# Down products with the activations stationary and 512 weight columns moving, a shorter delta rule, and the first norm moved ahead

## What is computed (the reference, cut)

```python
for i in range(2):                       # block i
    mod = silu(c) @ w_ada[i] + b_ada[i]  # 6 vectors of 1024: shift, scale, gate twice
    x += g1 * mixer_i(rms_norm(x) * (1 + sc1) + sh1)       # hgrn2, then rg-lru
    x += g2 * peer_ffn(rms_norm(x) * (1 + sc2) + sh2)      # 16384 experts, top 16 of 8 heads
x = rms_norm(x)
# even layer: gated delta rule (6 heads of 128, chunks) + windowed attention -> w_out, layer norm
# conv ffn: up (1024 -> 2*2816), conv over time, silu gate, down (2816 -> 1024), layer norm
# odd layer: differential attention + gated linear attention, layer norm; conv ffn, layer norm
```

## Time and profile before

| | us |
|---|---|
| median of 3 runs (lowest, highest) | 3236.56 (3231.42, 3238.88) |
| the profiled execution's own time | 3236.47 |
| its span, first to last instruction | 3234.8 |
| PE busy, PEld busy | 3014.2, 2896.0 |
| DVE busy, ACT busy, POOL busy | 2230.7, 1585.7, 79.8 |
| share of the ending chain: PE, DVE, ACT | 80%, 5%, 4% |

### The profile page before, as it was taken

One profiled execution on the slowest core, in us unless ns is written; L12 is line 12 of the kernel. 1 busy time (PEld: TensorE's weight loads), 2 busy tenths in 40 slices (PEclk: granted clock), 3 DMA queues, 4 the chain that ended last, 5 costly groups with the idle time before them and its releaser, 6 DMA issues.

```text
span 3234.8 us, 64227 instructions
## 1 busy us (share of the span) xinstructions
PE 3014.2 (93%) x22954; PEld 2896.0 (90%) x22954; DVE 2230.7 (69%) x4709; ACT 1585.7 (49%) x3278; POOL 79.8 (2%) x121
## 2 busy tenths in 40 slices
PE   4997999999999999899999999998997889898898
PEld 4886899999999998799999999998986789886898
DVE  5336479888779974459888867775675358763686
ACT  1110457778544432555777744445442148461574
POOL 2000000000001100000000000001100000000000
PEclk9998999999999998999999999998997899997999
DMA  8520455454478852345444455554330045431453
GB/s 320 221 94 1 149 177 168 152 163 141 156 261 303 300 170 98 124 163 187 153 150 160 141 187 184 186 188 164 120 118 1 14 156 180 163 118 52 143 177 122
DMA packets 137769, 503.50 MB, mean 156 GB/s; under 512 B 15328, under 2 KB 15456, under 8 KB 137344
## 3 DMA queue, kind: packets, MB, share of 16 engines
q1 hardware_dynamic: 122544, 445.57, 41.2%
q0 software_dynamic: 15056, 55.65, 4.8%
HBM read 499.05 MB, written 2.10 MB: 155 GB/s over the span
## 4 chain that ended last, share of the span: by engine, by line
PE 80%; DVE 5%; ACT 4%; issue 1%; DVEq 0%; ACTq 0%
PE PB L509 12%; PE PB L511 12%; PE PB L510 12%; PE PA L509 9%; PE PA L511 9%; PE PA L510 9%; PE PB L499 5%; PE PA L685 4%; DVE w_low L1974 1%; PE PA L885 1%; PE PB L885 1%; PE PA L1025 1%; DVE BIG L2000 1%; PE PA L590 1%; PE PB L582 1%
## 5 line engine op out<-in xcount | busy, mean ns | idle before, releaser
L1062 ACT ACTIVATE w_high<-ring 128x512 fp32r<-128x512 f32 x1484 | 924.4, 630 | 944.3 <-PE PA L511 498.1
L1974 DVE TENSOR_TENSOR w_low<-ring,w_high 128x512 fp32r<-128x512 f32 x1484 | 1014.6, 695 | 430.3 <-ACT w_high L1062 411.9
L509 PE MATMUL PB<-h_high,w_low 128*128 128x256 f32 x3536 | 1024.6, 290 | 44.9 <-DVE h_low L1653 36.9
L511 PE MATMUL PB<-h_high,w_high 128*128 128x256 f32 x3536 | 1003.4, 284 | 0.0
L510 PE MATMUL PB<-h_low,w_high 128*128 128x256 f32 x3536 | 1002.7, 284 | 0.0
L509 PEld LDWEIGHTS PB<-h_high,w_low 128*128 128x128 f32 x3536 | 685.4, 194 | 60.6 <-issue 47.8
L509 PE MATMUL PA<-a_high,w_low 128*128 128x256 f32 x2400 | 678.7, 283 | 10.2 <-DVE a_low L1983 10.1
L511 PE MATMUL PA<-a_high,w_high 128*128 128x256 f32 x2400 | 676.8, 282 | 0.0
L510 PEld LDWEIGHTS PB<-h_low,w_high 128*128 128x128 f32 x3536 | 676.6, 191 | 0.0
L511 PEld LDWEIGHTS PB<-h_high,w_high 128*128 128x128 f32 x3536 | 675.6, 191 | 0.0
L510 PE MATMUL PA<-a_low,w_high 128*128 128x256 f32 x2400 | 674.6, 281 | 0.0
(11 more groups left out here) (326 smaller groups left out, 2849.4 us busy)
## 6 DMA issues: line engine op xcount, KB each, us to landing
ring<-tiles SPq DMA_DIRECT2D x842, 512.0 KB, 3.3
BIG<-ada POOLq DMA_DIRECT2D x96, 512.0 KB, 7.9
BIG<-skew POOLq DMA_DIRECT2D x4, 512.0 KB, 4.5
X<-x SPq DMA_DIRECT2D x1, 1024.0 KB, 5.8
skew<-BIG POOLq DMA_DIRECT2D x1, 1024.0 KB, 6.8
out<-X SPq DMA_DIRECT2D x4, 256.0 KB, 2.0
con<-consts SPq DMA_DIRECT2D x1, 853.0 KB, 8.7
BIG<-masks POOLq DMA_DIRECT2D x1, 768.0 KB, 8.0
```

Of the source, the lines that this page charges most:

```text
L509: mm(dst, lhs_l, high, start=start, stop=False, skip_group_check=True)
L511: return mm(dst, lhs_h, high, start=False, stop=stop, skip_group_check=True)
L1062: fn(tile_half(w_high, s, b), ring[:, at:at + HALF], ACT.Identity).then_inc(sem("high_ready"), 1)
L1974: tt(tile_half(w_low, s, b), ring[:, at:at + HALF], tile_half(w_high, s, b).bitcast(F32), ALU.subtract).then_inc(sem("low_ready"), 1)
```

## The change

1. `split_sums`: the activations (128 tokens of `a_high` or `a_low`) are stationary and 512 weight columns move, so a tile takes 12 matmuls, not 24; the sums then lie with tokens on the partitions. At each of the four ends ACT and DVE copy the sums to SBUF (`TMP`), PE turns them back in 16 transposes (`turn_sums`) into PB, and the additions to X read PB.
2. The modulation groups 8 to 11 are summed by PE after the norm that follows the first `peer`, groups 6 and 7 where all six were. At the start of the program the first norm's sums, root and scaling come before ada group 1.
3. Delta rule: beta is folded into a key decay made in the tile loop (rows of beta by PE at tile 3, copied by ACT at tile 4; masks applied on DVE at tiles 9 to 15), so the matrix needs no turning and beta scaling afterwards. Squares of q and k and v's turning move into tiles 38 to 40. A level makes three groups of products for each half g, not four (the last level two), because the second is had by swapping the operands. The mask DMA, `nbeta` and the buffers n, nt, c, p2 go. The output part that needs no second delta is made earlier.

The diff, cut to its core:

```diff
@@ banks of the norms
-            return (PB if name in SUMS else PA)[:, i * 512:i * 512 + T]
+            return PA[:, i * 512:i * 512 + T]
...
@@ PE
             def split_sums(j, k, it, step, first=False, last=False):
                 pe.wait_ge(sem("gated_ready"), it * 4 + (j + 1))
+                high, low = pair(a_high, j), pair(a_low, j)
                 for b in range(2):
                     pe.wait_ge(sem("low_ready"), it * (2 * step) + (2 * k + b + 1))
-                    for q in range(4):
-                        m = 4 * b + q
-                        ins = passes(PA[:, m * T:(m + 1) * T], k, b, q, pair(a_high, j), pair(a_low, j),
-                                     first and m % 2 == 0, last)
+                    w_h, w_l = tile_half(w_high, k, b), tile_half(w_low, k, b)
+                    for t in range(TT):
+                        dst, own = PA[:, (t * 2 + b) * HALF:(t * 2 + b + 1) * HALF], slice(t * P, (t + 1) * P)
+                        mm(dst, high[:, own], w_l, start=first, stop=False, skip_group_check=True)
+                        mm(dst, low[:, own], w_h, start=False, stop=False, skip_group_check=True)
+                        ins = mm(dst, high[:, own], w_h, start=False, stop=last, skip_group_check=True)
                     ins.then_inc((sem("mid_tile"), tile_done)[b], 1)
+            def turn_sums():
+                pe.wait_ge(sem("sums_copied"), w.up(sem("sums_copied"), TT))
+                for m in range(DC):
+                    for t in range(TT):
+                        ins = nc.tensor.transpose(PB[:, m * T + t * P:m * T + (t + 1) * P],
+                                                  TMP[:, t * D + m * P:t * D + (m + 1) * P], ident)
+                    if m % 2:
+                        ins.then_inc(sem("sums_turned"), 1)
...
-                    ada(LATER, 12, PB)
+                    ada(LATER, LATER + 2, PB)
                 for j in range(4 * steps + 1, NKEYS):
                     down(j)
+                turn_sums()
...
+                    if j == 3:
+                        beta_rows()
...
+                    if j == n - 4:
+                        pe.wait_ge(sem("attention_out_taken"), 4 * TT)
+                        gdn_squares(0)
+                    if j == n - 3:
+                        gdn_values()
+                    if j == n - 2:
+                        gdn_squares(1)
...
                 for lev in range(1, PAIR_LEVELS):
+                    last = lev == PAIR_LEVELS - 1
                     for g in range(2):
-                        pe.wait_ge(sem("inverse_step"), w.up(sem("inverse_step")))
-                        times(PA, g, "ct", "x").then_inc(sem("inv_p1"), 1)
-                        times(PB, g, "c", "y").then_inc(sem("inv_p2"), 1)
+                        if lev == 1:
+                            pe.wait_ge(sem("inv_p1_ready"), copied - 1 + g)
+                        pe.wait_ge(sem("inverse_x"), 2 * (lev - 1) + g + 1)
+                        times(gdn_bank(g), g, "ct", "x").then_inc(sem("inv_p1"), 1)
+                    if lev == 1:
+                        pair_products(4)
+                        pair_products(5)
                     for g in range(2):
                         pe.wait_ge(sem("inv_p1_ready"), w.up(sem("inv_p1_ready")))
-                        times(PA, g, "y", "p1").then_inc(sem("inv_xpx"), 1)
-                        pe.wait_ge(sem("inv_p2_ready"), w.up(sem("inv_p2_ready")))
-                        times(PB, g, "x", "p2").then_inc(sem("inv_ypy"), 1)
+                        if lev == 1:
+                            pe.wait_ge(sem("pair_taken"), 5 + g)
+                        pe.wait_ge(sem("inverse_y"), 2 * (lev - 1) + g + 1)
+                        if not last:
+                            times(gdn_bank(g), g, "y", "p1").then_inc(sem("inv_xpx"), 1)
+                        times(gdn_bank(2 + g), g, "p1", "y").then_inc(sem("inv_ypy"), 1)
...
-            ada(0, 2)
-            pe.wait_ge(sem("mod_ready"), w.up(sem("mod_ready")))
             rms()
+            ada(0, 1, PB, False)
+            ada(1, 2, PB)
+            pe.wait_ge(sem("mod_ready"), w.up(sem("mod_ready")))
...
             rms("experts0")
-            linear("lru_x", H, sem("h_ready"))
+            ada(LATER + 2, 12, PB[:, 1024:])
+            linear("lru_x", H, sem("h_ready"), 0, 2)
+            pe.wait_ge(sem("mod_ready"), w.up(sem("mod_ready"), 2))
+            linear("lru_x", H, None, 2)
@@ ACT
+            def copy_sums(stream):
+                r0, n = STREAM_AT[stream]
+                act.wait_ge(tile_done, r0 + n)
+                fn(TMP[:, 0:D], PA[:, 0:D], ACT.Identity).then_inc(sem("sums_copied"), 1)
...
                 for j in range(n):
+                    if j == n - 1:
+                        gdn_values()
+                        head_roots(2 * GDN_HEADS, 1.0, GDN_SUMS)
...
+                    if j == 4:
+                        act.wait_ge(sem("gam_psum"), w.up(sem("gam_psum")))
+                        fn(e["rows"], PA[:, 0:12 * P], ACT.Identity).then_inc(sem("beta_rows_taken"), 1)
...
@@ DVE
                 dve.wait_ge(tile_done, r0 + n)
+                v.tensor_copy(TMP[:, D:2 * D], PA[:, D:2 * D]).then_inc(sem("sums_copied"), 1)
                 for m in range(DC):
-                    add_chunk(m, PA[:, m * T:(m + 1) * T], gate).then_inc(sem("x_added"), 1)
+                    if m % 2 == 0:
+                        dve.wait_ge(sem("sums_turned"), w.up(sem("sums_turned")))
+                    add_chunk(m, PB[:, m * T:(m + 1) * T], gate).then_inc(sem("x_added"), 1)
...
+                    if j in (9, 12, 15):
+                        key_decay(j // 3 - 3)
+                    if j in (11, 14):
+                        query_decay(j // 3 - 3)
...
-            ada(0, 2)
-            modulate(0, 2)
+            ada(0, 1)
             dve.wait_ge(sem("x_loaded"), w.up(sem("x_loaded"), 16))
             rms(None, H)
+            ada(1, 2)
+            modulate(0, 2, PB)
```

More of the change, by code:

```diff
@@ L389, in build, with gdn_bank, gdn_part @@
         GDN_PSUM = {x: i + 1 for i, x in enumerate(
-            ("values", "matrix", "turned", "delta0", "carry", "delta1", "out"))}
-        GDN_COPIED = {x: i + 1 for i, x in enumerate(("values", "matrix", "turned", "delta0", "delta1"))}
+            ("values", "delta0", "carry", "early", "delta1", "out"))}
+        GDN_COPIED = {x: i + 1 for i, x in enumerate(("values", "delta0", "delta1"))}
+        GDN_PAIRS = (("k", 0, 0), ("k", 1, 1), ("k", 0, 1), ("q", 0, 0), ("q", 0, 1), ("q", 1, 1))
+        GDN_SUMS = PA[:, 1536:1536 + T]
+        HALF_HEADS = GDN_HEADS * P
+        def gdn_bank(i):
+            return (PA, PB)[i // 2][:, i % 2 * 1024:i % 2 * 1024 + HALF_HEADS]
+        def gdn_part(name, g):
+            return EVEN[name][:, g * HALF_HEADS:(g + 1) * HALF_HEADS]
         REL, ONEHOT, ROWS = big(0, 512), big(512, SKEW), big(105 * T, 4 * SKEW)
@@ L551, in all_taken, with ada @@
                 pe.wait_ge(taken, q0 + n)
-            def ada(first, last, dst=PA):
+            def ada(first, last, dst=PA, done=True):
                 pe.wait_ge(sem("ada_sums_ready"), last)
@@ L749, in mixing, with beta_rows @@
                     ins.then_inc(sem("ba_psum"), 1)
+                def beta_rows():
+                    pe.wait_ge(sem("beta_ready"), w.up(sem("beta_ready")))
+                    for t in range(TT):
+                        for h in range(GDN_HEADS):
+                            i = t * GDN_HEADS + h
+                            ins = mm(PA[:, i * P:(i + 1) * P], wide(e["beta"][:, i:i + 1], P, P), ident,
+                                     start=True, stop=True)
+                    ins.then_inc(sem("gam_psum"), 1)
                 def gam_columns():
+                    pe.wait_ge(sem("beta_rows_taken"), w.up(sem("beta_rows_taken")))
                     pe.wait_ge(sem("g_ready"), w.up(sem("g_ready")))
@@ L878, in even_mixer @@
[L878 to L886 removed]
+                    spread_roots(2 * GDN_HEADS, 2 * at, (i % 4) * 512)
@@ new lines, in pair_products @@
+                def pair_products(i):
+                    name, s, t = GDN_PAIRS[i]
+                    if i >= 2:
+                        pe.wait_ge(sem("pair_taken"), i - 1)
+                    for h in range(GDN_HEADS):
+                        ins = mm(gdn_bank(2 + i % 2)[:, h * P:(h + 1) * P],
+                                 e["k"][:, h * T + s * P:h * T + (s + 1) * P],
+                                 e[name][:, h * T + t * P:h * T + (t + 1) * P], start=True, stop=True)
+                    ins.then_inc(sem("pair_psum"), 1)
@@ new lines, in block, with times @@
+                def block(name, i):
+                    return e[name][:, i * P:(i + 1) * P]
+                def times(dst, g, lhs, rhs):
+                    for i in range(6):
+                        ins = mm(dst[:, i * P:(i + 1) * P], block(lhs, 6 * g + i), block(rhs, 6 * g + i),
+                                 start=True, stop=True)
+                    return ins
```

(21 more changed lines are left out.)

283 lines of the change are left out of this document (137 added, 146 removed).

## The result

The changed kernel takes 3159.46 us (median of four runs, 3159.38 to 3161.32) against 3235.12 for the kernel before on the same chip: a ratio of 0.9765, 95% interval 0.975 to 0.9781. It is faster, by 76 us where 122 were forecast, and lies 1.5 us above the range. The execution profiled took 3161.32 us, span 3159.6, so its rows are compared with a span of 3234.8 before: 75.2 us.

What follows compares the result with a forecast made beforehand. PE was taken as the bound, busy 93% of the span and 80% of the ending chain. Terms -64 + 8 - 7.5 - 7.5 - 52 = -123 took 3236.47 us to 3114; range 3093 to 3158.

Steps and rivals of the forecast that it cites:

- Down products: Down stages: 512-column fp32r matmuls start 216 ns apart (bounds 213, 225), saving 53 us outside and 11 in ada tiles: -64.
- the 11 ns: Down stages: a 256-column matmul takes 117.7 ns where streaming needs 106.7; this extra staying per matmul gave the 225 bound.
- Rival A: Down products: extra time goes with the columns, 512 take 233 ns, stage gains 9 us, not 64: 3169; chance 0.11.
- The ada tiles: 72 down tiles with ada work: DVE comes next as limit, 2.70 us a tile instead of 2.857, -11 us.
- Turning back: Four ends of the down stages: copies, four transposes before the first addition and semaphores cost +8 us (bounds 5 and 13).
- the 275 ns: Skill's price for a PE transpose; at it the ends would cost some 5 us more; six in 0.82 us were traced.
- Modulation sums: Around the first down stage's end: 32 records stay, 64 move behind the norm; net -7.5 us (bounds -13 and -2).
- Start: Program start: first norm's work goes before ada group 1, first product at 47.95 instead of 55.61; -7.5 us (bounds -9, -4).
- Delta rule: Even mixer: fewer passes before level 1, six product groups a level instead of eight, shorter tail; -52 us (bounds -62, -35).
- (a): Delta rule, end of the tile loop: squares and v's turning in tiles 38 to 41 delay the roots, +1.3 us.
- Rival B: Delta rule: low clock and waits take the place of its products, half of 52 gained: 3140; chance 0.12.
- Rival C: Down matmuls: stationary loads not hidden, about 111 ns each, 400 us, slower than before: 3514; chance 0.03.

Runs made afterwards that it cites:

- part 1 alone: The kernel before with only the 512-column down products and the sums turned back at the ends: ratio 0.9984 to the kernel before, -5 us.
- the bf16 series: Program of matmuls alone, without the kernel's computation, 512 bf16 columns back to back: 215.8 ns from start to start.
- the fp32r series: Same program of matmuls alone, 512 fp32r columns, both operands at even places: 226.7 ns from start to start, with or without busy neighbours.
- part 2 alone: The kernel before with only the first norm's work moved ahead and 64 of 96 later modulation-sum records moved behind the next norm: ratio 0.9937, -20 us.
- the all-even one: The changed kernel with only its buffers reordered, so weights, activations and normed input start at the same place modulo 2048 bytes: 3161.92 us, ratio 0.9767.

## Why the prediction was wrong, point by point

**Down products: the failed step is "I take 216 ns".** The bounds above it (213 and 225) missed, too. The plain float32 record that stood as its model has 2.8 ns above its 512 steps (216.1 alone); an fp32r matmul has 13.3 ns at even places, and the kernel's places add 4.5. The remark that the 11 ns might stay with each matmul was the right mechanism, though as a bound too low. Measured, by the same sum: 228 tiles x 0.05 and 72 x 0.034 give -14 us, not -64 (the four stages of part 1 alone: -13). The 15 ns by 3600 matmuls are 54 us, more than the whole miss; the other terms gave some of it back. What the places add is measured; where the constant of 13.3 ns comes from is not shown. Rival A named the right time for a stage (233 ns, 3169) and had 0.11, but not for its reason: the extra does not go with the columns. That it comes so near in the time is luck of the places.
The Trainium skill (TensorE: Matmul & The Clock Gate, "Back-to-back issue gap") gives 215.8 ns for 512 columns; the bf16 series agrees to the tenth, the fp32r series, at 226.7, does not.

**The ada tiles.** DVE was to end them at 2.70 us; it was PE at 2.82.

**Turning back.** +8 was forecast (bounds 5 and 13). The distances from last down matmul to mean squares grew by 2.08, 2.79, 2.63 and 2.99 us: +10.5, within the bounds. Four transposes take 0.67 us. A transpose's record is 0.27 us long but for the first of a group, and the starts lie 0.109 apart. So the 275 ns that the prediction quotes, and says that the trace disagrees with, fit the length of a record; as a pace, which the sum needs, they do not fit.

**Modulation sums.** -7.5 forecast; -6.9 in the run with part 2 alone and -8.0 in the changed kernel against part 1 alone (down stage 366.1 us for 379.5; from the end of the mean squares to the lru product 9.76 for 4.3 before). 64 records take 9.76 us and not 10.8. One step of it was luck: the 32 records left in the down stage were to be "over before the clock fell". In the run with part 2 alone they were (1192.92 to 1196.4), but the clock fell at once behind them, with the narrow down matmuls 213 ns apart until 1200.8. In the changed kernel it fell within them, and a dozen wide matmuls at 427 ns lost some 2.4 us (12 x 0.196). The sum has no term for either.

**Start.** 47.98 for 47.95. The sums of group 1 began at 42.72 for 42.55.

**Delta rule.** -52 forecast, -56 (between the down stages) to -57 (by the ratio) measured. By pieces in the changed kernel: mean squares to roots 203.3 us for 200.0, +3.3 where +2.3 was counted with the work in the loop; roots to level 1 19.2 for 51.4, -32.2 for -32; levels 49.5 for 68.8, -19.3, as worked out; the tail 21.9 for 30.8, -8.9 for -3. In the tail the output products behind the last copy fell from 4.3 to 1.62 us, the copy and squares from 2.95 to 0.82, and the spread roots on the chain from 4.98 (12 records) to 1.14 (4 records); for those the granted clock was 0.56 before and 1.00 after, so a part of this gain is the clock's. The prediction also has an error of 1.3 us in its sum: the -32 runs from the old start of level 1 to the new one (2475 to 2443) and so already holds the +1.3 of (a), which is added once more. Rival B is refuted: PE is not idle between the groups of a level, though the clock was low through the roots, as it supposed. Rival C too: loads stay hidden.

**The sum by measured terms:** -13 (down products) + 10.5 (ends) - 8 (sums) - 7.6 (start) - 57 (delta rule) = -75, for 75.2 between the two profiled executions and 76 between the medians.

## What to carry to other kernels

Price a matmul form by a series of exactly that type, width and pair of buffers; a record of another type is no model for it. In this case, halving the count of fp32r matmuls at even places saved a constant of 13 ns for each one saved, and no more. Then look at where the two operands of the hot matmuls start: here 32 bytes and an order of allocation, with no instruction changed, gave 17 us or more, where the wide form had given 3 to 5. Read a stage's distances one by one before you take its mean for a price: ten at the lower clock made 227.8 of 226.7.

## What was unexpected of the hardware

The distance between fp32r matmuls depends on where their operands lie against each other: 512 columns took from 226.7 to 233.4 ns, 256 columns from 115.6 to 120.0, at the same clock, alike each time a pair was run again. At the lower level neither the constant nor the place shows: the wide matmuls start 427 ns apart (512 steps of 1.2 GHz are 426.7) in the changed kernel (1191.84 to 1196.5) as in the all-even one (1846.9 to 1849.8). The weight load is a suspect for the constant: its record is 190 ns long for fp32r and 98 for bf16, which has no such cost. But for plain float32 it is 190 ns, too, and a record takes 216.1; no run took the load away, so the cause stays open. A neighbour costs a streaming fp32r matmul nothing: VectorE and ScalarE at work without pause and DMA at 200 GB/s left 226.7 at 226.7. The later modulation sums (products with one column, two records for each) brought PE to its lower level, 1.2 GHz, within or right behind each group of 32 to 96 records; at which record differs from run to run. The granted clock in and behind the 64 records of the changed kernel:

```profile
1209.70:1219.40 9.70, 9.70 (x66) 9.70 (x64) 4.25 (x5) 4.51 (x9) 0.00 (x0) 0.70 0.01 2
1219.50:1224.00 4.50, 4.50 (x11) 3.60 (x12) 0.54 (x3) 3.78 (x6) 0.00 (x0) 0.51 0.00 0
1224.00:1240.00 16.00, 16.00 (x75) 14.06 (x75) 8.80 (x18) 0.81 (x1) 0.00 (x0) 1.00 0.38 133
```
